# Gathering expert rows before the last expert is done, and adding its rows by a matmul

## The reference, cut to what matters

```
for e in range(16):                       # each token has 2 experts with weight > 0
    h = silu(z @ w_gate[e]) * (z @ w_up[e])            # 1024 -> 512
    y = y + combine[:, e:e+1] * (h @ w_down[e])        # 512 -> 1024
out = layer_norm(ALPHA * z + y, ln2_g, ln2_b)
```

## Time and profile before

| | us |
|---|---|
| runs | 655.62, 654.79, 650.20 |
| median | 654.79 |
| profiled execution, first to last instruction | 655.5 |

### The profile page before, as it was taken

How to read it: one execution, slowest core, us unless ns; L and a number is a source line. 1 busy time by engine, 2 the same in 40 slices (tenths; PEclk the granted TensorE clock), 3 DMA queues, 4 the chain that set the end, 5 groups by cost and what they waited for, 6 DMA issues and landing times.

```text
span 655.5 us, 8986 instructions
## 1 busy us (share of the span) xinstructions
PE 527.6 (80%) x3529; PEld 388.7 (59%) x3530; DVE 224.4 (34%) x472; ACT 130.0 (20%) x240; POOL 71.6 (11%) x86
## 2 busy tenths in 40 slices
PE   1399979999999999999953899996877897788700
PEld 1399955887989788778653555543443453444300
DVE  5624976686432223014444111121011111111047
ACT  1424367843521212000110000000000000000010
POOL 4690300000000000010003400010000000000030
PEclk9999999978999999999955899999788998888855
DMA  7695632402157889870194299999999999999252
GB/s 219 199 247 172 163 113 65 129 1 65 36 189 222 285 283 300 295 253 1 59 379 161 72 379 380 378 387 387 387 387 388 390 388 387 396 397 396 85 169 80
DMA packets 84088, 158.52 MB, mean 242 GB/s; under 512 B 3572, under 2 KB 35792, under 8 KB 84048
## 3 DMA queue, kind: packets, MB, share of 16 engines
q1 hardware_dynamic: 74976, 135.11, 57.9%
q0 software_dynamic: 4784, 13.52, 7.5%
q10 hardware_dynamic: 4288, 9.31, 3.9%
HBM read 146.14 MB, written 11.78 MB: 241 GB/s over the span
## 4 chain that ended last, share of the span: by engine, by line
PE 50%; issue 19%; SPq 12%; DMA 10%; DVE 5%; ACT 2%; POOL 0%; POOLq 0%; DVEq 0%
PE bank L989 8%; PE bank L799 8%; PE bank L950 6%; PE bank L786 6%; PE bank L787 6%; PE bank L788 6%; SPq L576 5%; SPq L580 4%; DMA expert_slots<-in_w_up 4%; DMA expert_slots<-in_w_in 3%; PE bank L875 2%; SPq L575 2%; PE bank L768 1%; PE bank L769 1%; PE bank L855 1%
## 5 line engine op out<-in xcount | busy, mean ns | idle before, releaser
L989 PE MATMUL bank<-expert_slots,work 128*64 128x256 f32 (+3 forms) x1600 | 200.2, 424 | 37.2 <-DMA expert_slots<-in_w_up 17.0
L989 PEld LDWEIGHTS bank<-expert_slots,work 128*64 128x64 f32 (+1 forms) x1600 | 109.2, 141 | 117.1 <-issue 54.8
L786 PE MATMUL bank<-z_high,weights_high 128*128 128x320 f32 (+1 forms) x256 | 81.4, 318 | 0.4 <-DVE weights_low L516 0.4
L787 PE MATMUL bank<-z_low,weights_high 128*128 128x320 f32 (+1 forms) x256 | 80.1, 313 | 0.0
L788 PE MATMUL bank<-z_high,weights_low 128*128 128x320 f32 (+1 forms) x256 | 79.9, 312 | 0.0
L1658 DVE SCALAR_TENSOR_TENSOR work<-work,bank 128x256 f32<-128x256 f32 (+1 forms) x18 | 7.3, 407 | 158.8 <-ACT work L1234 152.9
L516 DVE TENSOR_TENSOR weights_low<-expert_slots,weights_high 128x2048 fp32r<-128x2048 f32 x18 | 41.4, 2299 | 32.9 <-ACT weights_high L511 32.8
L799 PE MATMUL bank<-work,expert_slots 128*128 128x320 f32 x192 | 52.3, 432 | 0.0
L786 PEld LDWEIGHTS bank<-z_high,weights_high 128*128 128x128 f32 x256 | 48.9, 191 | 1.5 <-DVE weights_low L516 0.7
L787 PEld LDWEIGHTS bank<-z_low,weights_high 128*128 128x128 f32 x256 | 48.6, 190 | 0.2
L788 PEld LDWEIGHTS bank<-z_high,weights_low 128*128 128x128 f32 x256 | 48.6, 190 | 0.0
(11 more groups left out here) (236 smaller groups left out, 573.5 us busy)
## 6 DMA issues: line engine op xcount, KB each, us to landing
expert_slots<-in_w_gate SPq DMA_DIRECT2D x16, 2048.0 KB, 20.9
expert_slots<-in_w_up SPq DMA_DIRECT2D x16, 2048.0 KB, 23.5
expert_slots<-in_w_down SPq DMA_DIRECT2D x16, 2048.0 KB, 21.0
expert_slots<-in_w_in SPq DMA_DIRECT2D x19, 1024.0 KB, 5.5
expert_slots<-in_w_branch_rnn SPq DMA_DIRECT2D x4, 1024.0 KB, 7.9
expert_slots<-in_w_out SPq DMA_DIRECT2D x4, 1024.0 KB, 6.4
expert_rows<-work ACTq DMA_DIRECT2D x32, 128.0 KB, 6.2
expert_rows<-work POOLq DMA_DIRECT2D x16, 128.0 KB, 3.8
```

Source lines behind the costliest of these rows:

```text
L786: nc.tensor.matmul(b[:, 0:NALL - lo], wh[:, k, o], zh[:, k, lo:NALL], start=(k == 0), stop=False)
L787: nc.tensor.matmul(b[:, 0:NALL - lo], wh[:, k, o], zl[k // 4][:, k % 4, lo:NALL], start=False, stop=False)
L989: mm = nc.tensor.matmul(bank[m * j:m * j + m, cols], lhsT(k), rhs(k, j), start=(k == 0), stop=(k == kk - 1))
```

## The change

The gathers no longer wait for the last expert. Expert 15's first 64 slots are not written to `expert_rows`; those rows of the DRAM tensor are left at zero. In their place:

- SP loads the last down matrix in two halves with a semaphore each; the sums over k wait for each half.
- DVE, after `down(14)`, builds for each choice a token-by-slot matrix (`own_rows`, 128 tokens x 3 tiles x 64 slots, written twice side by side): the token's weight where its item is 15 and its slot matches, zero elsewhere. The two choices are added. PE turns it (`turn_own`), ACT copies it to `own_T`.
- PE then runs `hidden(15)`, `turn_hidden` and `down_last`; ACT copies the result to `own_y` in SBUF, and PE multiplies `own_T` by it (`add_last`, six matmuls of 64 rows by 512 columns) into PSUM banks.
- The overflow items, when there are any, run ahead of expert 15 and not behind it.
- POOL waits for the row writes itself, does one tiny add, and issues the same six gathers, into the space of weight slot 2.
- DVE adds all three gathered tiles first (`add_gathered`), then per tile adds the two PSUM halves, and goes on with moments and norm as before.

The diff, cut to its core:

```
-        fin = Area(slots, 0, 3 * EXP)
+        fin = Area(slots, 2 * EXP, 3 * EXP)
+        own_rows = [xg[2][:, 384*k:384*k+384].rearrange("p (j h c) -> p j h c", h=2, c=FIRST) for k in range(2)]
+        own_T = xT[2].rearrange("p k c -> p (k c)")[:, 0:NTOK]
+        own_y = yo[2]
+        SUM = [[banks[0], banks[1]], [banks[3], banks[4]], [banks[5], banks[7]]]
...
 # SP
-            load_down(NE - 1, 0)
+            last_down = t["w_down"][0, LAST].rearrange("(k p) f -> p k f", p=P)
+            for h in range(2):
+                sp.dma_start(w_down[0][:, 2*h:2*h+2, :], last_down[:, 2*h:2*h+2, :]).then_inc(d_last[h], 16)
...
 # POOL
+            total = word(pool, W_TOTAL, NE)
+            pool.wait_ge(y_out[0], 32 * (NE // 3))
+            pool.wait_ge(y_out[2], 32 * (NE // 3))
+            pool.wait_ge(y_out[1], 32 * (count + NE // 3))
+            pool.wait_ge(yb_out, 16 + 64 * (count + total))
+            nc.gpsimd.tensor_tensor(idle, eps, eps, ALU.add).then_inc(y_written, 1)
             pool.wait_ge(y_written, 1)
+            pool.wait_ge(zero_out, 16 * NITEM)
...
 # PE
+            def turn_own():
+                pe.wait_ge(own_made, 1)
+                for j in range(3):
+                    n = OUT_ROWS[j]
+                    mm = nc.tensor.transpose(HB[2][:, P*j:P*j+n], own_rows[0][0:n, j].rearrange("p h c -> p (h c)"), ident[0:n, 0:n])
+                mm.then_inc(own_full, 1)
+            def add_last():
+                pe.wait_ge(own_turned, 1)
+                pe.wait_ge(ly_made, 1)
+                for j in range(3):
+                    n = OUT_ROWS[j]
+                    for h in range(2):
+                        half = slice(FIRST*h, FIRST*h + FIRST)
+                        mm = nc.tensor.matmul(SUM[j][h][0:n, :], own_T[half, P*j:P*j+n], own_y[half, :], start=True, stop=True)
+                    mm.then_inc(sum_full[j], 1)
...
-            down(NE - 2, 2, NE // 3 - 1)
-            hidden(NE - 1, 0, NE // 3)
-            maybe_rest(NE - 1, 0, NE // 3)
-            turn_hidden(NE - 1)
-            down(NE - 1, 0, NE // 3)
+            down(LAST - 1, 2, NE // 3 - 1)
             (overflow items)
+            turn_own()
+            hidden(LAST, 0, NE // 3, la_full)
+            (rest of the last expert, if any)
+            turn_hidden(la_made, 1, lt_full)
+            down_last()
+            add_last()
...
 # ACT
-            act.wait_ge(y_out[0], 32 * (NE // 3 + 1))
-            (waits for all other writes)
-            nc.scalar.copy(th_a[:, 0:1], ident[:, 0:1]).then_inc(y_written, 1)
+            act.wait_ge(own_full, 1)
+            nc.scalar.copy(own_T, HB[2][:, 0:NTOK]).then_inc(own_turned, 1)
+            gate_tanh(0, la_full, 1, la_tanh)
+            act.wait_ge(y_out[2], 32 * (NE // 3))
+            act.wait_ge(ly_full, 1)
+            nc.scalar.copy(own_y, YB[:, :]).then_inc(ly_made, 1)
...
 # DVE
+            dve.wait_ge(ya_full, LAST)
+            places = [place[:, 3*k:3*k+3] for k in range(4)]
+            for k in range(2):
+                step(stt(own[:, k, :], places[k], float(LAST), weight[k], ALU.is_equal, ALU.mult))
+            step.settle()
+            slots_of = cst("iota_cap")[:, 0:FIRST].unsqueeze(1).to_broadcast([P, 2, FIRST])
+            for k in range(2):
+                for j in range(3):
+                    step(ts(own_rows[k][:, j], slots_of, places[2+k][:, j:j+1], own[:, k, j:j+1], ALU.is_equal, ALU.mult))
+            step.settle()
+            tt(own_rows[0][:, :], own_rows[0][:, :], own_rows[1][:, :], ALU.add).then_inc(own_made, 1)
+            (silu and hidden_columns of the last expert)
             dve.wait_ge(rows_scaled2, 3)
+            for j in range(3):
+                add_gathered(j)        # wait yg_in[j], then the two multiply-adds of before
             for j in range(4):
                 if j < 3:
-                    dve.wait_ge(yg_in[j], 32)
-                    (two multiply-adds of the gathered rows)
+                    dve.wait_ge(sum_full[j], 1)
+                    for h in range(2):
+                        half = rows[0:n, j, 512*h:512*h+512]
+                        step(tt(half, half, SUM[j][h][0:n, :], ALU.add))
+                    step.settle()
                     moments(j, n)
                 if j > 0:
                     normed(2, j - 1, OUT_ROWS[j - 1])
```

More of the change, by code:

```diff
@@ L386, in build @@
         weight = [sm.take(3) for _ in range(2)]
+        place = sm.take(12)
+        own = sm.take(2, 3)
+        idle = sm.take(1)
         exi, exo = rt.take(15), rt.take(15)
@@ L470, in build @@
         y_written = sem("y_written")
+        la_full, la_tanh, la_half, la_made = [sem(f"last_hidden_{n}") for n in ("full", "tanh", "half", "made")]
+        lt_full, lt_made, ly_full, ly_made = [sem(f"last_{n}") for n in ("turned", "turned_made", "down", "down_made")]
+        d_last = [sem(f"down_last{i}") for i in range(2)]
+        own_made, own_full, own_turned = sem("own_made"), sem("own_full"), sem("own_turned")
+        sum_full = [sem(f"sum_full{j}") for j in range(3)]
         yg_in = [sem(f"yg_in{j}") for j in range(3)]
@@ L1037, in round_of @@
                     i = 3 * n + s
-                    hidden(i, s, n)
+                    hidden(i, s, n, ha_full)
                     if not (first and s == 0):
@@ L1700, in _, with add_gathered @@
                     hidden_columns(v + NE)
+            dve.wait_ge(ha_made, LAST + count)
+            dve.wait_ge(ya_full, LAST)
+            places = [place[:, 3 * k:3 * k + 3] for k in range(4)]
+            for k in range(2):
[4 more added lines that the diff above has]
+                for j in range(3):
+                    step(ts(own_rows[k][:, j], slots_of, places[2 + k][:, j:j + 1], own[:, k, j:j + 1], ALU.is_equal, ALU.mult))
+            step.settle()
+            tt(own_rows[0][:, :], own_rows[0][:, :], own_rows[1][:, :], ALU.add).then_inc(own_made, 1)
+            def add_gathered(j):
+                n = OUT_ROWS[j]
+                dve.wait_ge(yg_in[j], 32)
+                for k in range(2):
+                    alone(stt(rows[0:n, j, :], yg[j][k][0:n, :], weight[k][0:n, j:j + 1], rows[0:n, j, :], ALU.mult, ALU.add))
+            silu(1, th_a, hid_a, HB[0][:, 0:256], HB[0][:, 256:512], la_tanh, la_half, la_made)
+            has, b = rest_words(dve, LAST)
+            with dve.If(has > 0):
+                rest(b + count)
+            dve.wait_ge(lt_full, 1)
+            V.tensor_copy(hT_a, TH[:, 0:256]).then_inc(lt_made, 1)
             dve.wait_ge(rows_scaled2, 3)
+            for j in range(3):
+                add_gathered(j)
             for j in range(4):
```

114 lines of the change are left out of this document (63 added, 51 removed).

## The result

The changed kernel runs in 651.09 us (median of 20 runs, 645.43 to 653.93) against 654.14 us for the kernel before (20 runs, 649.14 to 658.4): ratio 0.995, 95% interval 0.9927 to 0.9974. That is 3.3 us faster (1.7 to 4.8), where 7.3 were forecast. The profiled execution took 652.22 us with a span of 650.4, so 1.8 us lie around the span, not 0.1.

A forecast was written before the change was run, and what follows sets the result against it. Weights pace the expert stage, then a serial chain runs; gathers starting at 612.4, gathered adds until 628.9 and 16.0 us more end DVE at 644.9, not 652.2. That 7.3 us off 654.79 gives 647.5 us, range 643.0 to 654.0.

The forecast's parts named there:

- DVE's stretch behind the last gathered add: PSUM adds, moments and norms on DVE after the gathered adds: 16.0 us, ending at 644.9 instead of 652.2.
- the wait for tile 1: DVE adds gathered tile 0 until 622.3, then waits for tile 1 at 623.6.
- The base: The 7.3 us gain, worked out on one execution of 655.6 us, was subtracted from the median, 654.79: 647.5.
- The start of the gathers: On POOL: expert 14's rows land at 612.0, plus 0.4 us; first gather at 612.4, 12.65 us earlier.
- The gathers' flow: Gathers keep their spacing: tile 0 whole 6.4 us after the first start, tile 1 after 11.2, tile 2 about one more.
- The extra zeros lie in the first 60 us.: The added block of zeros, early in the kernel, was listed among what costs nothing.
- the branch over the overflow items: On PE behind down(14): costs nothing, since PE waits for DVE there anyway.
- A: PE's chain is the bound: with own rows taking 5.5 us, tile 0's sum comes at 630.7; time 649.3; chance 0.2.
- B: PE at half clock from 605.5 to the end, hidden(15) 13.8 us: no gain, or up to 658.5; chance 0.07.
- C: Row writes or gathers late: landing at 615.7 moves the gathered adds by 3.7 us: 651.2; chance 0.15.
- D: POOL's gathers held by DVE's instructions between 612.4 and 620, 2.6 us in all: 650.1; chance 0.05.
- E: Expert 14's row writes land at once, at 609.2: time 643.9 to 645.9; chance 0.08.

The follow-up runs named there:

- before_again: The kernel before, unchanged, run and profiled again: ratio 0.9995 to the kernel before, tail 60.5 us.
- after_again: The changed kernel, unchanged, run and profiled again: ratio 0.9949 to the kernel before, tail 57.5 us.
- upstream_only: The kernel before plus only the extra zeros, place in the small tile and the last down matrix loaded in halves: ratio 1.0042 to the kernel before.
- no_jump: The changed kernel without PE's branch and code for overflow items, which this data lacks: 649.39 us in one run.
- after_warm_2: The changed kernel with matmuls of no use filling PE's gaps, second run of it: ratio 0.9895 to the kernel before.
- zero_moved_2: The changed kernel with POOL's sixth 384 KB block of zeros issued behind the router's loads, second run: ratio 0.9929 to the kernel before.
- own_early: The changed kernel with the token-by-slot matrices built in a free place without waiting for down(14): ratio 0.9955 to the kernel before.

## Why the prediction was wrong

**What held.** The mechanism and its order: the gathered rows are the bound, PE has some slack, DVE's stretch behind the last gathered add took 647.01 - 631.02 = 16.0 us as worked out, and the wait for tile 1 came where it was put. The size was off, in four terms:

**1. The base.** The sum took 7.3 us off one execution, and the prediction laid that against the median taking that execution for the run of 655.6 us. With the 1.8 to 1.9 us around the span that every later profile has, it took about 657.3 us; 9 of 139 runs of before are that long. Its tail of 62.2 us is 1.3 above the mean of six. Both its down steps had a low stretch of the clock, but the one on down(14) does it: the first gather came 35.1 us after the tail's start and not 33.4 as in before_again, whose down(15) was slow too. The prediction saw the stretches in its rows ("the idling also costs clock") and charged one to the new kernel's PE, where it doesn't matter, but didn't ask how often before pays them on its path: it subtracted from an execution that pays more than the mean. That is 1.3 of the 7.3. (In the changed kernel the stretch on down(14) costs less: the first gather of after_again is 0.8 us later for it.)

**2. The start of the gathers.** "I take 0.4 us" from landing to first gather; it took 613.92 - 612.81 = 1.1 us. The POOL add is 0.19 us, but 0.57 lie between it and the gather and 0.3 ahead of it. The landing itself was mis-sized as well, but made up for: the later of the two writes took 6.7 us and not 5.5, so it landed 7.9 us after down(14) ended and not 6.5, while down(14) mostly ends 1.7 us sooner than in the execution that the sum was read from. The first gather came 22.8 us after the tail's start, where the forecast's 612.4 is 22.4; over the five profiles of the change's order it is 23.2. The term costs 0.8.

**3. The gathers' flow.** DVE could start on tile 1 11.9 us after the first gather (11.87 here, and the mean of the five is the same), not 11.2: 0.7 us more, directly on DVE's path.

By the tails these three make 7.3 - 1.3 - 0.8 - 0.7 = 4.5 us, against 4.6 seen.

**4. "The extra zeros lie in the first 60 us."** I costed them at nothing and named no cover. Loads of weights run beside them, and PE waits 0.73 us on average for a unit that is late. All parts ahead of the tail together cost 0.1 to 0.7% (upstream_only), 0.7 us of it seen in the rows. 4.6 us in the tail less 0.7 are 3.9, and 3.3 (1.7 to 4.8) was measured. This fourth term is the least sure: no run of the zeros alone is clear of no change.

One cover named in the prediction failed without a price: the branch over the overflow items doesn't stand beside DVE's work alone. Where down(14) is short PE comes to the turn 1.3 us after DVE's matrices are there (3.95 against 2.65), and hidden(15) started 4.9 us after down(14) ended, not 2.8. This goes off the 1 to 2 us that PE's chain has to spare.

What stays open: the share of the zeros in upstream_only's loss (alone they gave 1.0026 and 1.0004, and to move one block back didn't clearly return anything), whether the matmuls of no use help the changed kernel, and what lets some executions keep the full clock from 120 to 200 us.

**The rivals.** A (PE the bound) is not the cause: after_again's sums were done 5.3 us before they were needed and its tail was no shorter. In no_jump and after_warm_2 PE's chain was the last by a little; both tails, 55.5 and 55.8 us, are below the mean. B (slower by half clock) didn't come: hidden(15) took 9.2 us, not 13.8. C (late landing): the rows landed 7.3 us after the first issue, between the 5.9 that the sum took and C's 9.6, but 21.7 us after the tail's start, where the sum has 22.0. D: the sixth gather ran beside the end of DVE's silu and the fifth beside its start, and they took no longer than the first:

```profile
618.93 0.92 POOL L756 DMA_INDIRECT expert_slots<-expert_rows,slot_i  x1 [0.30 <-issue]
620.15 0.91 POOL L756 DMA_INDIRECT expert_slots<-expert_rows,slot_i  x1 [0.31 <-issue]
```

In zero_moved_2 the sixth gather ran beside DVE's copy of the hidden rows and took no longer either:

```profile
618.75 0.42 DVE L1786 COPY work<-bank 128x256 f32<-128x256 f32 x1 [1.05 <-PE bank L1038]
618.88 0.91 POOL L757 DMA_INDIRECT expert_slots<-expert_rows,slot_i  x1 [0.30 <-issue]
```

So no hold by DVE is seen. The Trainium skill, SBUF — State Buffer, section "Who interferes with whom", names copy, cast and tensor_scalar as steps that can enter a two-port mode, under conditions; of DVE's steps beside the gathers only this copy is of that kind, and the rows don't say in which mode it ran, so the rule itself isn't tested here. The own matrices took DVE 607.49 - 605.0 = 2.5 us, against 2.1; that was off the path. E (landing at 609.2) didn't come.

## What to carry to other kernels

Before subtracting a sum from a median, ask where the profiled execution lies among the runs, and which of its terms are chance: here a low stretch of the clock on down(14) was worth 1.7 us of the old path, a short one on down(15) next to nothing, and a gain read from an execution that has both is more than the mean gain. A write added to the DMA queues can make a neighbour wait, here PE by 0.7 us on average, 500 us ahead of the place that was changed: look at who loads beside it. When the runs of one kernel fall into two kinds, find where they part before reading tenths of a per cent. And when data stay on chip to allow an overlap, price the two apart: here keeping them cost 7 to 8 us and overlapping gave back 11.

## What the runs showed of the hardware that I had not expected

- PE took 3.95 us from the end of down(14) to the next matmul with all its inputs ready (own_early); without the register loads and the branch over the unused overflow items it came 2.65 us behind down(14), with DVE's result (no_jump, one run). With a down(14) of 5.35 us the gap was 2.65 us with the branch in place (after_again).
- On POOL 0.57 us passed between the end of a tiny add and an indirect DMA that waited for it; between two gathers in a row it is 0.30.
- POOL's add behind expert 14's row writes came 6.4 to 7.6 us after their first issue, beside a weight stream of 396 GB/s in 602 to 604 us of the first profile. Expert 15's writes in before's order, when that stream was over, landed 2.2 to 3.6 us after their issue.
- The same stage (120 to 200 us) got a granted clock of 1.00 in some executions and of 0.89 in others, with PE busy for over 98% of it in all.
- The time of a run lies 1.8 to 1.9 us above the span of its profile, in every profile taken here.
